# A weight ring of eight slots instead of six, in a transformer block with a mixture of experts

## The reference

```python
mod = silu(c) @ ada_w + ada_b                    # 1024 x 6144
sh1, sc1, g1, sh2, sc2, g2 = split(mod, 6)
h = rmsnorm(x, norm1_g) * (1 + sc1) + sh1
xr, gr, u, v = split(h @ w_in)                   # 1024 x 2048
y_lru = rg_lru(causal_conv(xr), ...) * gelu(gr)
y_sgu = spatial_gating(gelu(u), gelu(v), ...)
x = x + g1 * (concat([y_lru, y_sgu]) @ w_out)    # 1024 x 1024
h = rmsnorm(x, norm2_g) * (1 + sc2) + sh2
# each token: the best of 4 groups, and in it the best 2 of 8 experts
y = sum_over_chosen(weight * (silu(h @ w1[e]) * (h @ w3[e])) @ w2[e])
x = rmsnorm(x + g2 * y, final_g)
```

## Time and profile before

| what | value |
|---|---|
| median of 3 runs | 964.03 us (963.91 to 966.81) |
| the profiled execution's own time | 963.78 us |
| its span, first to last instruction | 962.0 us |
| PE busy | 886.4 us (92%) |
| DVE, ACT, POOL busy | 414.9, 310.9, 36.8 us |
| mean granted TensorE clock | 0.979 |
| transfers | 291.42 MB, 303 GB/s over the span |
| the experts' loads | 96 of 2048 KB |
| the mixer's loads | 18 of 2048 KB (one in two halves) |

### The profile page before, as it was taken

How to read it: one execution, slowest core, us unless ns; L and a number is a source line. 1 busy time by engine, 2 the same in 40 slices (tenths; PEclk the granted TensorE clock), 3 DMA queues, 4 the chain that set the end, 5 groups by cost and what they waited for, 6 DMA issues and landing times.

```text
span 962.0 us, 12747 instructions
## 1 busy us (share of the span) xinstructions
PE 886.4 (92%) x5348; PEld 581.1 (60%) x5348; DVE 414.9 (43%) x781; ACT 310.9 (32%) x564; POOL 36.8 (4%) x23
## 2 busy tenths in 40 slices
PE   4999999999899889988989998899999998999995
PEld 2668864434444424444334433698889898888985
DVE  3187961111111101110111100587877867788772
ACT  4352141111111101111101110666267555725652
POOL 0001000000000000000000000011110001110000
PEclk9999999999999999999999999999999999999998
DMA  9999787999999999999999999353334245233321
GB/s 386 422 427 377 292 318 324 427 399 427 429 427 426 431 427 425 429 426 427 427 429 429 427 426 424 128 184 124 132 109 155 89 154 203 105 132 132 132 88 44
DMA packets 24538, 291.42 MB, mean 303 GB/s; under 512 B 2720, under 2 KB 2976, under 8 KB 4000
## 3 DMA queue, kind: packets, MB, share of 16 engines
q1 hardware_dynamic: 24480, 290.58, 73.4%
HBM read 289.52 MB, written 1.05 MB: 302 GB/s over the span
## 4 chain that ended last, share of the span: by engine, by line
PE 50%; DMA 29%; DVE 13%; ACT 5%; issue 2%; SPq 1%; DVEq 0%; ACTq 0%
DMA ring<-in_expert_w 27%; PE bank L914 15%; PE bank L1280 15%; PE bank L333 4%; PE bank L943 3%; DVE lo L1226 3%; DMA ring<-in_ada_w 2%; DVE X L303 2%; PE bank L348 1%; PE bank L375 1%; PE bank L1310 1%; ACT hi L1220 1%; PE bank L869 1%; PE bank L263 1%; PE bank L892 1%
## 5 line engine op out<-in xcount | busy, mean ns | idle before, releaser
L914 PE MATMUL bank<-ring,xg 128*64 128x512 f32 x1024 | 244.3, 608 | 30.9 <-DMA ring<-in_expert_w 29.7
L914 PEld LDWEIGHTS bank<-ring,xg 128*64 128x64 f32 x1024 | 77.4, 140 | 194.7 <-issue 146.6
L1280 PE MATMUL bank<-HH,hi 128*128 128x256 f32 x432 | 129.1, 299 | 12.0 <-DVE lo L1226 9.1
L1280 PE MATMUL bank<-HL,hi 128*128 128x256 f32 x432 | 123.5, 286 | 0.0
L1280 PE MATMUL bank<-HH,lo 128*128 128x256 f32 x432 | 123.3, 286 | 0.0
L943 PE MATMUL bank<-ring,X 128*64 128x512 f32 x512 | 114.5, 600 | 0.7 <-ACT X L983 0.7
L1034 DVE TENSOR_TENSOR X<-X,bank 128x512 f32<-128x512 f32 x16 | 11.0, 688 | 239.7 <-PE bank L914 239.7
L1280 PEld LDWEIGHTS bank<-HH,hi 128*128 128x128 f32 x432 | 84.0, 194 | 19.2 <-issue 10.2
L1226 DVE TENSOR_TENSOR lo<-raw,hi 128x1024 fp32r<-128x1024 f32 (+1 forms) x86 | 93.0, 1116 | 2.3 <-ACT hi L1220 2.3
L1220 ACT ACTIVATE hi<-raw 128x1024 fp32r<-128x1024 f32 (+1 forms) x94 | 87.1, 975 | 11.0 <-DMA raw<-in_units 10.9
L1280 PEld LDWEIGHTS bank<-HL,hi 128*128 128x128 f32 x432 | 84.0, 195 | 1.1 <-issue 1.0
(11 more groups left out here) (331 smaller groups left out, 1337.5 us busy)
## 6 DMA issues: line engine op xcount, KB each, us to landing
ring<-in_expert_w SPq DMA_DIRECT2D x96, 2048.0 KB, 17.3
raw<-in_units SPq DMA_DIRECT2D x42, 1024.0 KB, 4.8
ring<-in_ada_w SPq DMA_DIRECT2D x12, 2048.0 KB, 14.1
ring<-in_w_in SPq DMA_DIRECT2D x3, 2048.0 KB, 32.8
ring<-in_w_out SPq DMA_DIRECT2D x2, 2048.0 KB, 9.9
ring<-in_w_in SPq DMA_DIRECT2D x2, 1024.0 KB, 22.0
scr<-in_b SPq DMA_DIRECT2D x1, 1536.0 KB, 35.2
cst<-in_cst SPq DMA_DIRECT2D x1, 1536.0 KB, 14.7
```

The costliest lines, as they stand in the source:

```text
L914: t = pe.matmul(bank[3 + i][64 * x:64 * x + 64, :], xg[q % 2][:, k, o + 64 * x:o + 64 * x + 64], place(at[x])[:, k, :], start=k == 0, stop ...
L1280: t = pe.matmul(ps[:, T * j:T * j + T], part(st), part(mv), start=first and a == 0, stop=last and a == 2, skip_group_check=True)
```

## The change

The ring gets eight slots. Six lie where they did. Slot 6 and slot 7 (`more`) lie over tensors that aren't in use while the slots are: the late constants (now a tensor of their own, `late`), `X3`, `rs`, `rt`, `rows`, `yT` and `X2`. Loads 0 to 17 take their slots from a table, the experts' loads go round the eight; each load waits for the last use of the load before it in its own slot, and the first that takes slot 7 (load 22) for the end of the last projection (`s_proj` 18). Slot 6 has no first wait (load 6). What the mixer kept in the overlaid tensors while slots 6 and 7 are filled moves: the router's weights to the end of `scr`, the last two rows of `mod` to `hT`, `acc` and `ac` to the end of `X2`. The arrival semaphores of the units become those of the ring's slots. The first four units wait for the last use of the slots over which they lie, and the late constants, which lie in slot 6, for the last use of that. The four clearing products and the memset behind them go: the first product of the first scatter on each bank starts the sum instead. The second block's count for `s_fill` goes down by the memset's one.

```diff
-NS = 6
+NS = 8
...
-        cst = sb("cst", NCONST)
+        cst = sb("cst", EARLY)
...
+        late, X3, rs, rt, rows, yT, X2 = overlay(late=(NCONST - EARLY,), X3=(3, 256), rs=(2, T), rt=(T,), rows=(1024,), yT=(8, T),
+                                                 X2=(3, 384))
+        (more,) = overlay(more=(2, 4096))
+        sb("both", NCONST - EARLY + 768 + 512 + 256 + 1024 + 2048 + 1152)
...
-        (ring,) = overlay(ring=(NS, 4096))
+        (ring,) = overlay(ring=(NS - 2, 4096))
...
-        slot_of = [n % NS for n in range(len(stream))]
+
+        slot_of = [3, 2, 0, 4, 5, 1, 6, 3, 2, 4, 5, 0, 6, 1, 2, 3, 4, 5]
+        slot_of += [(0, 6, 1, 2, 7, 3, 4, 5)[n % NS] for n in range(len(stream) - 18)]
...
+            slot = ring[:, slot_of[n], :] if slot_of[n] < 6 else more[:, slot_of[n] - 6, :]
+            return slot[:, 0:k * w].rearrange("p (k n) -> p k n", k=k)
+
+        FIRST = 6
...
             for n in range(first, last):
-                sp.wait_ge(*freed(n - NS))
+                held = [m for m in turns_of[slot_of[n]] if m < n]
+                if held:
+                    sp.wait_ge(*freed(held[-1]))
+                elif slot_of[n] == 7:
+                    sp.wait_ge(s_proj, 18)
                 sp.dma_start(place(n), stream[n]).then_inc(s_ring[slot_of[n]], 16)
...
             if i >= 10:
-                act.wait_ge(s_ln, 14)
+                act.wait_ge(s_htT, 4)
...
             if n == 0:
                 pe.wait_ge(s_modc, 24)
-                pe.wait_ge(s_fill, 5)
-                for a in range(4):
-                    pe.matmul(bank[ACC[a]][:, :], none, cst[0:32, 0:512], start=True, stop=False)
...
                         t = pe.matmul(bank[ACC[a]][:, T * k:T * k + T], part(y[:, d:d + 128]), part(PT[n % 2][:, :]),
-                                      start=False, stop=n == NP - 1 and k == 1 and j == 1)
+                                      start=n == 0 and k == 0 and j == 0, stop=n == NP - 1 and k == 1 and j == 1,
+                                      skip_group_check=True)
...
-            if first == 0:
-                dve.memset(none, 0.0).then_inc(s_fill, 1)
...
-        stream_sp(NS, first_load(1))
+        stream_sp(FIRST, first_load(1))
...
         for U in range(4):
-            sp.wait_ge(s_up, 31 + U // 2)
-            sp.dma_start(unit_place(U), unit_source(U)).then_inc(s_load[U], 16)
-        sp.dma_start(cst[:, EARLY:], p["cst"][:, EARLY:]).then_inc(s_late, 16)
+            sp.wait_ge(*freed(max(turns_of[U])))
+            sp.dma_start(unit_place(U), unit_source(U)).then_inc(s_ring[U], 16)
+        sp.wait_ge(*freed(max(turns_of[6])))
+        sp.dma_start(late[:, :], p["cst"][:, EARLY:]).then_inc(s_late, 16)
```

More of the change, by code:

```diff
@@ L83, in build @@
         rstd = sb("rstd", T)
-        rs = sb("rs", 2, T)
-        rt = sb("rt", T)
         longest = ctx.enter_context(nc.sbuf_tensor("longest", [128, 1], mybir.dt.int32))
-        X1, X2 = sb("X1", 3, 384), sb("X2", 3, 384)
-        X3 = sb("X3", 3, 256)
-        rows = sb("rows", 1024)
+        X1 = sb("X1", 3, 384)
         rw = sb("rw", 9, 36)
         crep = sb("crep", 8, 32)
-        (ring,) = overlay(ring=(NS, 4096))
+        late, X3, rs, rt, rows, yT, X2 = overlay(late=(NCONST - EARLY,), X3=(3, 256), rs=(2, T), rt=(T,), rows=(1024,), yT=(8, T),
[3 more added lines that the diff above has]
+        (ring,) = overlay(ring=(NS - 2, 4096))
         raw0, hi0, raw1, hi1, raw2, hi2, raw3, hi3, HH, HL, YH, YL = overlay(
@@ L106, in con @@
             at, w = CONST[name]
-            return cst[:, at + a:at + (w if n is None else a + n)]
+            src, at = (cst, at) if at < EARLY else (late, at - EARLY)
+            return src[:, at + a:at + (w if n is None else a + n)]
         def v3(a, j):
@@ L135, in build @@
             stream += [p["expert_w2"][x].rearrange("p (k n) -> p k n", k=4) for x in (e, e + 1)]
-        slot_of = [n % NS for n in range(len(stream))]
+        slot_of = [3, 2, 0, 4, 5, 1, 6, 3, 2, 4, 5, 0, 6, 1, 2, 3, 4, 5]
+        slot_of += [(0, 6, 1, 2, 7, 3, 4, 5)[n % NS] for n in range(len(stream) - 18)]
         turns_of = [[n for n in range(len(stream)) if slot_of[n] == i] for i in range(NS)]
         s_ring = [sem(f"s_ring{i}") for i in range(NS)]
-        s_load = [sem(f"s_load{i}") for i in range(4)]
         def unit_place(U):
@@ L145, in unit_source, with unit_arrival @@
             return p["units"][U // NU, U % NU][:, 0:1024 if U % NU == U_ROWS else 2048]
+        def unit_arrival(U):
+            return s_ring[U % 4], 16 * (len(turns_of[U % 4]) + U // 4 + 1)
         def arrival(n):
@@ L193, in build @@
         mrow = X1[:, :, :].rearrange("p a n -> p (a n)")[:, 0:1024].rearrange("p (a n) -> p a n", a=2)
-        acc = [flat(X2[:, :, :])[:, 512 * i:512 * i + 512] for i in range(2)]
+        acc = [flat(X2[:, :, :])[:, 128 + 512 * i:640 + 512 * i] for i in range(2)]
         L = small[:, 64:136].rearrange("p (i n) -> p i n", i=2)
-        rwS, biasrow = flat(X3[:, :, :])[:, 0:288].rearrange("p (k n) -> p k n", k=8), flat(X3[:, :, :])[:, 288:324]
-        bvec = flat(X3[:, :, :])[0:1, 324:360]
+        rwS, biasrow = scr[:, 11400:11688].rearrange("p (k n) -> p k n", k=8), scr[:, 11688:11724]
+        bvec = scr[0:1, 11724:11760]
         tcol = small[:, 164:166]
         trow = small[:, 166:168]
-        late_rows = v3(rows[:, :], 2)
+        late_rows = v3(flat(hT[:, 0:4, :]), 2)
         shift = modc[:, 24:32]
@@ L208, in build @@
         sg, aT = flat(X1[:, :, :])[:, 0:512], v3(flat(X1[:, :, :])[:, 512:1024], 4)
-        ac = flat(X2[:, :, :])[:, 0:512]
-        none = rstd[0:32, 0:128]
+        ac = flat(X2[:, :, :])[:, 640:1152]
         weight = [small[:, 216 + s:217 + s] for s in range(2)]
@@ L227, in place @@
             k, w = stream[n].shape[1], stream[n].shape[2]
-            return ring[:, slot_of[n], 0:k * w].rearrange("p (k n) -> p k n", k=k)
+            slot = ring[:, slot_of[n], :] if slot_of[n] < 6 else more[:, slot_of[n] - 6, :]
+            return slot[:, 0:k * w].rearrange("p (k n) -> p k n", k=k)
+        FIRST = 6
         def first_sp():
             sp.dma_start(cols[:, :], p["cols"]).then_inc(s_cols, 16)
-            sp.dma_start(cst[:, 0:EARLY], p["cst"][:, 0:EARLY]).then_inc(s_cst, 16)
+            sp.dma_start(cst[:, :], p["cst"][:, 0:EARLY]).then_inc(s_cst, 16)
             sp.dma_start(xT[:, :, :], p["x"]).then_inc(s_x, 16)
-            for n in range(NS):
+            for n in range(FIRST):
                 if n == W_IN[0]:
@@ L1218, in high @@
                     U, (src, hi, _) = split_of(*divmod(N, len(PIECES)))
-                    act.wait_ge(s_load[U % 4], 16 * (U // 4 + 1))
+                    act.wait_ge(*unit_arrival(U))
                     act.activation(part(hi), src, ACT.Copy).then_inc(s_hi, 1)
@@ L1244, in second_sp @@
                     sp.wait_ge(s_unit, U - 3)
-                    sp.dma_start(unit_place(U), unit_source(U)).then_inc(s_load[U % 4], 16)
+                    sp.dma_start(unit_place(U), unit_source(U)).then_inc(s_ring[U % 4], 16)
                 for i in range(4):
@@ L1998, in conv_in @@
                     dve.wait_ge(s_rs, RS[l])
-                    dve.wait_ge(s_fill, l + 6)
+                    dve.wait_ge(s_fill, l + 5)
                     dve.wait_ge(s_unit, U + 1)
```

1 line of the change is left out of this document (removed).

## The result

The changed kernel took 957.64 us (median of 5 executions, 954.87 to 959.39), the kernel before 964.14 beside it (5 executions, 963.91 to 966.81): a ratio of 0.9926 [0.9901, 0.995]. The forecast was 953.4, with a range to 957.0, so the measured median lies 0.6 us outside. The profiled execution was the shortest of the five, 954.87 us, with a span of 953.1 and a mean granted clock of 0.981.

The account below looks back on a forecast made before the run. Transfers were taken to bound the first 600 us, with DMA engines standing still before the experts' long middle. The sum -9.8 + 0.1 - 0.8 = -10.5 from 963.78 gave 953.3, said as 953.4, range 951.0 to 957.0.

Parts of the forecast that it names:

- The place and the mechanism: Around the experts' start: two more slots put loads 24 and 25 before the 150.40 us release, every later load two places earlier.
- the loads' term: Experts' loads from 26 on: each lands two places earlier, 2 x 4.89 = 9.8 us, less 0.1 for the late load 25.
- The register read: On SP behind the wait for `longest`, before load 24: taken as 0.9 us, with bounds of zero and 10.6 us.
- Rival A: Register read before loads 24 and 25 is long: each us beyond 140.6 costs one; 958.6 at half range; chance (partly) 0.08.
- The clearing products: Pair 1, line 885: without them it ends 6.9 us earlier, but that buys only the gap at 201 us, 0.8 us.
- Rival B: Pair 1's clearing stretch was on the path: its 6.9 us, less the 0.8 already counted, come on top, 947.3; chance 0.05.
- The gap's term: Short DMA gap at 201 to 203 us, closed by the shorter pair 1: 0.8 us, with nothing lost after 203.
- PE's waits: PE's waits for the ring's loads: 29.7 us become 29.7 - 10.5 + 6.9 = 26 us, so PE stays second.
- Crowding out (C): Mixer's start: early loads delay those PE waits for by up to 14.7 us, giving 968.1; chance 0.02.
- D: The loads' gain is made, but the second block starts no earlier or runs longer by as much; about 963.5; chance 0.05.
- the last step of the sum: -10.5 against the profiled 963.78 gives 953.3; that execution is 0.25 below the median, so 953.3 to 953.6.
- what follows keeps its length: From the second block's first group, line 1280, starting at 601 instead of 611.4 us: the rest takes as long as before.

Follow-up runs that it names:

- r4: The changed kernel, but loads 24 and 25 wait for the first group of expert products, as before the change: 965.31 us, ratio 0.9993.
- g4: The changed kernel with loads 24 and 25 issued before SyncE's wait for `longest` and its register read: 955.02 us, ratio 0.9885.
- r3: The kernel before, with its six slots, without the four clearing products and their memset: 965.58 us, ratio 0.9993.
- r1: The changed kernel, not altered, timed again: 955.22 us, ratio 0.989 to the kernel before.
- e8: The changed kernel once more, not altered: 955.16 us, ratio 0.9902 to the kernel before.
- f4: The changed kernel, not altered, third repetition: 955.15 us.
- r2: The changed kernel's table and eight slots, with the clearing products, their memset and their wait put back: 958.59 us, ratio 0.9936.
- f3: The changed kernel plus extra products: four in the early wait, three in the last pair's wait, two and one of 256 columns before the second block: 951.83 us.
- g1: The kernel before, not altered, run for a second profile: 966.71 us, one profiled execution.
- g2: The kernel before, not altered, run for a third profile: 963.68 us, one profiled execution.
- e6: The changed kernel plus eight extra products where TensorE waits for its third piece of ada_w, 20.2 to 24.4 us: 959.23 us, ratio 0.9931.

## Why the prediction was right and wrong

**The place and the mechanism were right.** Two loads more in front of the release at 150.4 us, worth 2 x 4.89 us: r4 takes exactly these two away and the time is the old one. The last pair's second group came 9.8 us earlier, and 10.8 counted from the experts' start, against 10.5 forecast. That the total fits so well is in part luck: the loads' term is smaller than 9.7 (8.8 to 9.3) and the gap's larger than 0.8.

**The register read** was taken as 0.9 us between 0 and 10.6. It is inside the 0.8 us from DVE's cast to the issue. Rival A falls, by this row and by g4.

**The clearing products** were hidden but for the gap, as forecast, and the slow clock in pair 1 went with them (r3: 0.9993 [0.998, 1.0006] in the kernel before). Rival B falls. The gap's term was mis-sized: I read it from 201 to 203 us and wrote that nothing is lost after 203, but the rate stays low for another microsecond, and it is worth 1.6 us. PE's waits were to become 26 us and are 28.6.

**Crowding out (C)** falls: the first long wait ends at 3.74 + 20.68 = 24.4 us against 24.2. (Behind the load that this wait is for stood two loads and one half, not the two halves and one load of the prediction; that makes its case against C stronger.) **D** falls too: what the loads gave is there at the start of the second block, up to 1.6 us.

**What failed is the last step of the sum, "so a median of 953.3 to 953.6".** It took a profiled execution of 963.78 us and a median of three as the kernel's typical time. Over all runs of the study the kernel before has a median of 966.2 (59 executions, 963.7 to 969.6), and only 10 of the 59 are under 964.1. The changed kernel has 955.6 (22 executions, 954.1 to 960.0). That is 10.6 us, 1.1%, and my sum was 10.5: 966.2 - 10.5 = 955.7. In each series by itself the gain was 10.6 (r1), 10.0 (e8) and 11.5 us (f4). The difference was right and the level was 2 us too low. The result of 957.64 lies above the changed kernel's usual time as well: of the four executions above 957.5 that the 22 hold, three were among its five.

**With it failed "what follows keeps its length",** and the same for what comes before the experts. The first expert product moved from 143.28 to 144.29 us, the last group from 7.09 to 8.68, and the forecast for the span was missed by 1.6 us (953.1 for 951.5). Both are stretches in which TensorE was at the 1.2 GHz level for a time in one execution and at the full clock in another. For the last group that isn't only scatter: it takes 7.09 us in all three profiles of the kernel before and 8.68 to 8.79 in four of five of the changed kernel, behind a wait of 2.70 us in both first profiles. r2 with the eight slots alone, r3 without the clearing products alone, and r4 have 8.79 too, one profile each, so it can't be put down to either part. I had seen such a stretch in pair 1 and reckoned with it there, and had not asked where else PE stands still before work that is on the path. f3 shows that these stretches cost time: with three waits filled, 951.83 us for 955.15.

By the Trainium skill (TensorE: Matmul & The Clock Gate, Part 1) the number of slow products differs from run to run of one kernel, and the cost is below 1% of a typical span. g1 and g2 agree, with 3.0 us of 965, 0.3%. That is small, and still twice what the forecast of the span was off by.

**What stays open.** No execution of the changed kernel of 959 to 960 us was profiled, so where the longest ones lose 4 to 5 us isn't shown. The clock is the likely place: the four executions above 957.5 us have mean granted clocks of 0.974 to 0.977, the eleven fastest of the 22 have 0.978 to 0.983. A mean lower by 0.006 over 955 us is some 11 us more at the 1.2 GHz level (an estimate), enough for 4 to 5 us of lost time. But that is two things going together, and not a cause shown. What a slow last group costs is open too: r1's was fast and ended no earlier. Of the 3.4 us between r2 and r1, the gap that r2 keeps accounts for 1.3, by (429 - 318) / 429 x 5. r2's one profile shows its last group 1.4 us later and its second block 1.3 us longer than in the changed kernel's; the second is of the size that the clock moves between executions of one program, and whether the clearing products cause it wasn't tried with more profiles.

## What to carry to other kernels

In this kernel the ring that stood still cost by the loads that were missing in front of the next release: count those and multiply by the time of one; when exactly they left made no difference that could be seen. A forecast against one profiled execution should be told as a difference first, since the level of one execution or three can be off by more than the terms that one argues about. Where an engine's clock can fall, go through the waits of that engine on the path and ask of each what runs right behind it; short filling there may be worth more than the work removed elsewhere, but only if it ends before the data arrives.

## What the runs showed that I had not expected

- The granted clock fell to 0.50 with PE busy: eight records that fill 32 of 128 rows took 4.05 us, and from 189 to 195 us the clock was 0.50. Without them it is 1.00 (changed kernel, r3); with them put back (r2) it is 0.69 from 185 to 196 us, as r2's stretches show:

```profile
185.00:196.00 11.00, 11.00 (x38) 6.13 (x37) 1.16 (x3) 1.03 (x3) 0.00 (x0) 0.69 1.01 429
```

- A product of 512 columns over all 128 columns of the array takes 0.88 to 0.92 us (7.03 / 8 in e6, 2.77 / 3 in f3), two records each. The experts' products, in two halves, take 13.95 us for 64 records, 0.22 a record.
- SyncE stalled in an issue more often with the deeper ring, as the prediction had allowed. Before, one in the first 15 us took 4.17 us; now two long ones follow each other, and PE's first long wait ends only 0.2 us later. SyncE's timeline in the changed kernel:

```profile
6.88 4.12 SPq L251 DMA_DIRECT2D rw<-in_rw  x1
11.04 3.61 SPq L260 DMA_DIRECT2D more<-in_ada_w  x1
```
